# Low-rank decay input: sixteen columns taken out of the split-weight stream and multiplied in native fp32 over four column groups

## The reference, cut to what matters

```
h = modulate(rms_norm(x, norm_mix[i]), sh2, sc2)
z = h @ w_in[i]                       # 1024 x 8208 columns
ca, cb, q, k, v, r, a_lr, g_conv, g_gla = jnp.split(z, split_idx, axis=-1)
u = ca * jax.nn.sigmoid(cb)
d, conv_new = causal_depthwise_conv(u, conv_state[i], conv_w[i], conv_b[i])
log_a = jax.nn.log_sigmoid((a_lr @ w_alpha[i] + b_alpha[i]).astype(jnp.float32)) / GLA_TAU
```

## Time and profile before

| | us |
|---|---|
| median of three runs | 1552.81 |
| lowest, highest | 1550.1, 1555.76 |
| the profiled execution | 1552.72 |
| its span, first to last instruction | 1551.1 |
| PE busy in it | 1451.4 (94%) |
| DVE busy | 825.3 (53%) |
| ACT busy | 487.0 (31%) |

### The profile page before, as it was taken

How to read it: one execution, slowest core, us unless ns; L and a number is a source line. 1 busy time by engine, 2 the same in 40 slices (tenths; PEclk the granted TensorE clock), 3 DMA queues, 4 the chain that set the end, 5 groups by cost and what they waited for, 6 DMA issues and landing times. The chain is left out here.

```text
span 1551.1 us, 30240 instructions
## 1 busy us (share of the span) xinstructions
PE 1451.4 (94%) x11934; PEld 1399.7 (90%) x11934; DVE 825.3 (53%) x1381; ACT 487.0 (31%) x660; POOL 73.5 (5%) x108
## 2 busy tenths in 40 slices
PE   6999999999997998999998895899979999999996
PEld 5899999999997998998998895799979999999995
DVE  5323322332256685798795977775453343333345
ACT  5322122212235223433232233522252212222233
POOL 6100000000010000000000000000000000000000
PEclk9999999999999999999898998899989999999997
DMA  9754545454554223222323333322312322322311
GB/s 311 235 168 154 172 152 173 147 178 142 170 189 147 84 81 113 72 93 79 130 93 122 105 123 132 137 83 88 103 55 82 104 85 82 108 82 84 99 61 55
DMA packets 134277, 189.03 MB, mean 122 GB/s; under 512 B 3516, under 2 KB 114512, under 8 KB 134159
## 3 DMA queue, kind: packets, MB, share of 16 engines
q1 hardware_dynamic: 113436, 114.57, 23.3%
q0 software_dynamic: 16704, 64.75, 12.5%
q10 hardware_dynamic: 4050, 8.53, 1.5%
HBM read 174.37 MB, written 14.41 MB: 122 GB/s over the span
## 5 line engine op out<-in xcount | busy, mean ns | idle before, releaser
L1322 DVE TENSOR_TENSOR w_lo<-raw,w_hi 128x1024 fp32r<-128x1024 f32 x218 | 266.8, 1225 | 589.6 <-ACT w_hi L962 589.4
L548 PE MATMUL pu<-h_hi,w_hi 128*128 128x260 f32 x2480 | 508.1, 286 | 19.4 <-DVE w_lo L1322 10.5
L548 PE MATMUL pu<-h_hi,w_lo 128*128 128x260 f32 x2480 | 501.5, 284 | 0.0
L548 PE MATMUL pu<-h_lo,w_hi 128*128 128x260 f32 x2480 | 500.8, 284 | 0.0
L962 ACT CAST w_hi<-raw 128x1024 fp32r<-128x1024 f32 x218 | 227.9, 1046 | 682.3 <-PE pu L548 670.6
L548 PEld LDWEIGHTS pu<-h_hi,w_hi 128*128 128x128 f32 x2480 | 384.5, 190 | 27.5 <-issue 10.9
L548 PEld LDWEIGHTS pu<-h_lo,w_hi 128*128 128x128 f32 x2480 | 384.4, 190 | 0.0
L548 PEld LDWEIGHTS pu<-h_hi,w_lo 128*128 128x128 f32 x2480 | 384.3, 189 | 0.0
L1617 DVE SCALAR_TENSOR_TENSOR d<-u,cw,d 128x512 f32<-128x512 f32 x240 | 162.9, 747 | 0.0
L548 PE MATMUL pu<-f_hi,w_hi 128*128 128x260 f32 x704 | 143.0, 284 | 2.0 <-DVE f_lo L1571 2.0
L548 PE MATMUL pu<-f_hi,w_lo 128*128 128x260 f32 x704 | 141.8, 283 | 0.0
(11 more groups left out here) (260 smaller groups left out, 1242.3 us busy)
## 6 DMA issues: line engine op xcount, KB each, us to landing
raw_a<-in_w_ada POOLq DMA_DIRECT2D x32, 1024.0 KB, 7.8
raw<-in_w_in SPq DMA_DIRECT2D x30, 1024.0 KB, 5.3
raw<-in_ffn_up SPq DMA_DIRECT2D x22, 1024.0 KB, 5.3
raw<-in_ffn_gate SPq DMA_DIRECT2D x21, 1024.0 KB, 5.3
raw<-in_ffn_down SPq DMA_DIRECT2D x16, 1024.0 KB, 5.1
raw_a<-in_w_ada_final POOLq DMA_DIRECT2D x8, 1024.0 KB, 7.4
gates_d<-sg ACTq DMA_DIRECT2D x24, 260.0 KB, 2.0
raw<-in_ffn_down SPq DMA_DIRECT2D x8, 768.0 KB, 4.5
```

Of the source, the lines that this page charges most:

```text
L548: last = mm(pu[p][:, e, 0:HALF], w[p][:, k, :], m[:, k, e * HALF:(e + 1) * HALF], start=(k == 0 and j == 0), stop=(k == k_tiles - 1 and j ...
L1322: V.tensor_tensor(w_lo[p][:], raw[:, slot, :, p * P:(p + 1) * P], w_hi[p][:].bitcast(F32), ALU.subtract).then_inc(s_lo, 1)
```

## The change

`a_lr` leaves the sequence of units. Its 16 columns of `w_in` are loaded once, unsplit, into a tile `wa` of 8 k-tiles by 32 columns (16 of them zero), by one DMA that stands in SP's queue between the first feed-forward block and the conv loads. After the last conv unit PE multiplies `wa` in native fp32 (`a_rows`): k-tile k goes to column group k % 4 of the array, with the high and the low part of the activation in turn. Each group leaves its own partial sum in its own 32 PSUM partitions. ACT copies all 128 rows at once, and the logits product, whose `w_alpha` now stands four times in `walpha` with zero rows between, adds the four partial sums. POOL therefore clears `walpha` and issues four small DMAs in place of one. The four places of alr, their two weight loads, their splits on ACT and DVE and PE's wait on the last PSUM evacuation are gone.

```
-                        + [("conv", 16), ("alr", 4), ("qk", 8), ("v", 8), ("gates", 24),
+                        + [("conv", 16), ("qk", 8), ("v", 8), ("gates", 24),
...
-        walpha, alr = work[0:RANK, 0:HEADS * DK], work[0:RANK, HEADS * DK:HEADS * DK + N]
+        walpha, alr = work[:, 0:HEADS * DK], work[:, HEADS * DK:HEADS * DK + N]
+        wa = sb("wa", [P, KT, CG])
...
             ffn(1)
+            sp.wait_ge(s_wz, 1)
+            sp.dma_start(wa[:, :, 0:RANK], w_in[:, W_IN["a"]:W_IN["a"] + RANK].rearrange("(k p) n -> p k n", p=P)
+                         ).then_inc(s_wa, 16)
             with sp.Fori(0, 4) as i:
                 pair(Lin(at["conv"], 4, i), w_in, i * 256 + W_IN["cb"], (w_in, i * 256 + W_IN["ca"]))
-            pair(Lin(at["alr"]), w_in, W_IN["a"], (w_in, W_IN["a"]))
...
             pool.wait_ge(s_done, at["conv"])
-            pool.dma_start(walpha, A["w_alpha"][0]).then_inc(s_ld["wa"], 16)
+            nc.gpsimd.memset(walpha, 0.0).then_inc(s_wz, 1)
+            pool.wait_ge(s_wz, 2)
+            for g in range(4):
+                pool.dma_start(walpha[CG * g:CG * g + RANK, :], A["w_alpha"][0]).then_inc(s_ld["wa"], 16)
...
-            n = at["alr"]
-            pe.wait_ge(s_evac[1], n // 2)
-            unit(Lin(n), 0, h_hi, h_lo, done=4)
+            def a_rows():
+
+                pe.wait_ge(s_wa, 16)
+                pe.wait_ge(s_cve, KT)
+                for r in range(2):
+                    for j, m in enumerate((h_hi, h_lo)):
+                        for e in range(2):
+                            for g in range(4):
+                                last = mm(pg[CG * g:CG * (g + 1), 2 + e, 0:HALF], wa[:, 4 * r + g, :],
+                                          m[:, 4 * r + g, e * HALF:(e + 1) * HALF].bitcast(F32), start=(r == 0 and j == 0),
+                                          stop=(r == 1 and j == 1), tile_position=(0, CG * g))
+                last.then_inc(s_ao, 1)
+
+            a_rows()
...
-            n = at["alr"]
-            act.wait_ge(s_done, n + 1)
-            for e in (1, 0):
-                nc.scalar.copy(alr[:, e * HALF:(e + 1) * HALF], pu[0][0:RANK, e, 0:HALF]).then_inc(s_evac[e], 2)
-
-            for c in range(2):
-                act.wait_ge(s_raw[1], Lin(n).half().half().value(16, 16))
-                act.sem_inc(s_hi, 1)
-            for c in range(2, 4):
-                act.wait_ge(s_lo, n + c + 1)
-                step(Lin(n + c))
+            act.wait_ge(s_ao, 1)
+            nc.scalar.copy(halves(alr), pg[:, 2:4, 0:HALF]).then_inc(s_alr, 1)
...
             V.memset(c_f[:], 0.0).then_inc(s_cf, 1)
+            V.memset(wa[:], 0.0).then_inc(s_wz, 1)
...
-            n = at["alr"]
-            for c in range(2):
-                dve.wait_ge(s_raw[1], Lin(n).half().half().value(16, 16))
-                dve.wait_ge(s_hi, n + 3 + c)
-                dve.sem_inc(s_lo, 1)
-            for c in range(2, 4):
-                step(Lin(n + c))
```

More of the change, by code:

```diff
@@ L297, in decoder_step @@
         s_xsp, s_xr = sem("x_rows_spilled"), sem("x_rows_restored")
+        s_wz, s_wa = sem("w_a_cleared"), sem("w_a_loaded")
+        s_ao, s_alr = sem("a_rows_in_psum"), sem("a_rows_ready")
         s_lg, s_z, s_az = sem("logits_ready"), sem("z_ready"), sem("abs_z_ready")
@@ L746, in _ @@
                         state_transposes(4 * (c - 2))
-            n = at["alr"]
-            pe.wait_ge(s_evac[1], n // 2)
-            unit(Lin(n), 0, h_hi, h_lo, done=4)
+            def a_rows():
[10 more added lines that the diff above has]
+            a_rows()
             def u_tails():
-                pe.wait_ge(s_cve, KT)
-                pe.wait_ge(s_evac[1], at["alr"] // 2)
+                for p in range(2):
+                    pe.wait_ge(s_evac[p], at["qk"] // 2)
                 for t in range(KT):
@@ L763, in logits @@
                 if h == 0:
-                    pe.wait_ge(s_evac[0], at["alr"] // 2 + 2)
-                    pe.wait_ge(s_ld["wa"], 16)
+                    pe.wait_ge(s_alr, 1)
+                    pe.wait_ge(s_ld["wa"], 16 * 4)
                     pe.wait_ge(s_cts, 1)
@@ L1642, in _ @@
             conv.end(3)
-            n = at["alr"]
-            for c in range(2):
-                dve.wait_ge(s_raw[1], Lin(n).half().half().value(16, 16))
-                dve.wait_ge(s_hi, n + 3 + c)
-                dve.sem_inc(s_lo, 1)
-            for c in range(2, 4):
-                step(Lin(n + c))
             def sample_conv():
-                dve.wait_ge(s_evac[0], at["alr"] // 2)
-                dve.wait_ge(s_evac[1], at["alr"] // 2)
+                dve.wait_ge(s_evac[0], at["qk"] // 2)
+                dve.wait_ge(s_evac[1], at["qk"] // 2)
                 dve.wait_ge(s_cve, KT)
```

## The result

The changed kernel takes 1542.1 us (median of five runs, 1540.23 to 1545.06); the kernel before takes 1552.81 us in the same comparison (five runs, 1550.1 to 1559.12). The ratio of the two is 0.9922, with a 95% interval from 0.9899 to 0.9945: by the ratio 12 us less, and between 8.5 and 15.7; by the two medians 10.7 us less. In two later comparisons the ratio was 0.9911 (0.989 to 0.9933) and 0.9919 (0.9906 to 0.9933). The forecast was 1543.0 us.

The account below looks back on a forecast made before the run. PE, busy 94% of the span, sets the pace; the window shrinks from 19.51 us to 0.19 + 3.78 + 5.77 = 9.74, saving 9.77 from 1552.81: 1543.0 us, 8-in-10 range 1540.2 to 1546.8.

Parts of the forecast that it names:

- the window: End of last conv unit to end of first qk unit: 9.74 us in place of 19.51, saving 9.77.
- both waits: PE's idles around the alr unit, for the last PSUM evacuation (3.16 us) and first qk weights (3.25 us), both removed.
- the length of the stretch ahead: Sign: the stretch before the window (480 to 581 us) keeps its length to some tenths.
- change of form: PE switching between full-width units and `a_rows`: 0.09 us ahead and 0.10 us behind, 0.19 us added.
- the early slabs: Modulation weight slabs in the trace of before: sixteen matmuls take 1.86 us, so the 32 added ones take 3.78 us.
- the serial rival: Column groups do not overlap in `a_rows`: 15.6 us for the 32 matmuls, 1554.9 us in all; chance 0.03.
- The bound of 0.5 us for the load of `wa`: SP's queue: packets four times as dear would make the next load 1.5 us late for a cast; taken as 0.
- The 0.8 us kept for the range: POOL's `walpha` memset after the first feed-forward block: at most 0.8 us if DVE must stand still; taken as 0.
- The clock's loss in the window of before: First qk unit runs partly at 1.2 GHz, 7.25 us instead of 5.77: 1.48 us, removed by the change.
- The logits, costed at 0: Logits matmuls with 128 rows instead of 16, same 260 moving columns and matmul count: no change, 0 us.
- those that gave time back: Partly given back: lower clock level, memset and load hits in later stages cost 4.3 us, 1547.3 us; chance 0.12.
- DVE's 3.0 us of slack: DVE runs out of work 3.0 us before the first qk unit ends, so no wait returns in the v stage.

Follow-up runs that it names:

- the first repeated comparison: The changed kernel run again with no edit, beside the kernel before: 1541.83 us (six runs), ratio 0.9911 (0.989 to 0.9933).
- The second and third profile: The kernel before profiled twice more with no edit: single times 1552.38 and 1553.82 us, against 1552.81 us median of its first comparison.

## Why the prediction was right

**The path.** PE sets the pace, the window is where the change acts, and both waits go. Window 9.57 us, worked out 9.74; the same in three profiles. Of the signs, the length of the stretch ahead was claimed to some tenths. It is 0.5 us longer in the first profile of the change, and its end moves by 2.6 us over three profiles of that one program, so that sign was set too tight.

**The added matmuls.** 3.65 us with the change of form behind, worked out 3.78 + 0.10. The 1.86 us of the early slabs run to the first row of the next form, so they hold the change of form behind them; doubled, with 0.10 added, it was counted three times. The excess is 0.2 us. The 0.465 us for a group of four had it inside too; it is 0.44 with 260 columns. The 0.49 us for one logits matmul, and so the 15.6 us of the serial rival, is too large in the same way (see the logits below). Four groups overlap 3.98 times (one group against four). The Trainium skill's "TensorE: Matmul & The Clock Gate", Part 3, has 2.38 times for three groups, from which some 3.2 for four had been estimated; the measurement decides for nearly 4 in this form. The change of form itself cost 0.09 us ahead, as in the earlier trace rows. The bound of 0.5 us for the load of `wa` is not worked out: the same sentence has the load 1.5 us late. Nothing came of it.

**What was costed at 0.** The load of `wa` landed after 4.2 us, before the next weight load, and the conv loads are issued as before (453.44 us, 453.52 in the earlier trace rows). The memset on POOL lies beside DVE's residual on the path, and holds nothing up. The two timelines, POOL and DVE of the changed kernel:

```profile
471.00 0.53 POOL L498 MEMSET work<- 128x512 f32 x1 [10.79 <-PE pu L556]
```

```profile
470.97 0.49 DVE L1487 SCALAR_TENSOR_TENSOR x<-pu,mod,x 128x260 f32<-128x260 f32 x1 [0.30 <-PE pu L556]
471.38 0.47 DVE L1489 SCALAR_TENSOR_TENSOR x<-pu,mod,x 128x252 f32<-128x252 f32 x1
471.76 0.16 DVE L1491 TENSOR_TENSOR t<-pu,mod 128x8 f32<-128x8 f32 x1
```

In the kernel before, without a memset, the same three DVE operations take 0.49, 0.47 and 0.16 us. The 0.8 us kept for the range did not come. The Trainium skill's "SBUF — State Buffer", under "Who interferes with whom", has the exclusive lock for VectorE instructions in a 2-port perf mode, and says of those with two SBUF inputs that they contend with a GpSimd instruction that reads SBUF, not with one that only writes it. A memset only writes, and the trace agrees for these three operations.

**Where the size was off.** The saving was worked out as 9.77 us; the medians give 10.7 and the later ones 11.9 and 13.8 (1541.21 against 1555.04). Two terms were too small. That the forecast, 1543.0 us, still came within a microsecond of 1542.1 is in part luck: the three runs it started from have the lowest median of the kernel before, 1552.81 us, where the later comparisons have 1553.6 to 1555.0.

- The clock's loss in the window of before. I took 1.48 us, from one execution. The second and third profile have 3.1 and 4.2 us (the alr unit 7.39 and 8.49 us instead of 5.85, the qk unit 7.37 instead of 5.77). With the mean of three windows, 20.98 - 9.57 = 11.4 us. The prediction did see that one of two like waits was followed by the lower level and the other not, and drew from it only that later stages may differ, not that the window itself does.
- The logits, costed at 0. The step "a 16-row matmul takes no less than a 128-row one" is right for the matmuls and leaves out what stands round them. In the changed kernel four of them take 597.64 to 599.20:

```profile
597.40 0.40 PE L556 MATMUL pu<-h_hi,w_lo 128*128 128x260 f32 x2
597.64 1.92 PE L790 MATMUL pg<-work 128*128 128x260 f32 x8
599.20 0.59 PE L556 MATMUL pu<-h_hi,w_hi 128*128 128x260 f32 x2
599.63 0.40 PE L556 MATMUL pu<-h_lo,w_hi 128*128 128x260 f32 x2
```

From the last pair ahead to the second pair behind, that is 2.23 us, against 2.61 in the earlier trace rows (606.87 to 609.48): 0.4 us less. Narrow windows show single records. In the kernel before the second and the last of the eight are

```profile
607.52 0.38 PE L770 MATMUL pg<-work 16*128 16x260 f32 x1
608.83 0.38 PE L770 MATMUL pg<-work 16*128 16x260 f32 x1
```

and in the changed kernel the second and the sixth

```profile
597.86 0.38 PE L790 MATMUL pg<-work 128*128 128x260 f32 x1
598.74 0.38 PE L790 MATMUL pg<-work 128*128 128x260 f32 x1
```

That is 0.22 us a record in both, 1.31 over six steps and 0.88 over four: the matmuls themselves take 0.44 us each with 16 rows as with 128. The 0.4 us lies at the two ends. Before, the step to the first record is 0.32 us where a pair takes 0.24, the second record starts 0.33 us after the first, the next form 0.31 us after the last, and its first pair takes 0.34 us: 0.08 + 0.11 + 0.09 + 0.10 = 0.38. The 2.23 us now are the eight records and two steps of pairs, with nothing added. So what was saved is a change of form, from the units' 128 rows to 16 and back; with 128 rows the logits have the form of the units. I had counted such a change for `a_rows` and not the two that disappear. In the profile with one column group the logits have 32 rows, and run from 608.63 to 610.58, 1.95 us, as with 16.

The logits stand twice in the qk stage, and the second saving is partly spent in the wait of the late qk units: by the low parts of the weights, the two traces move 0.5 us further apart over the stage.

11.4 + 0.5 = 11.9 us, which is the saving of the first repeated comparison; as the three comparisons differ by 3 us, that is agreement within the noise and no more. What is left of the difference in the rest (948.6 to 950.6 us in three profiles before, 946.8 to 948.0 in three after, so 1.2 us on average beyond the logits) lies within what the same program shows; that all of it is chance is not shown.

**The rivals.** None of those that gave time back came true: behind the window PE has the same 29 waits before and after, 64.8 to 66.5 us in sum before and 65.2 to 66.8 after, and DVE's 3.0 us of slack (measured 2.9) held.

## What to carry to other kernels

A narrow product in a pipeline built for wide ones costs more in its places in the pipeline than in its matmuls: here 6.4 us of waits and 1.5 to 4.2 us of clock, beside 5.85 us of matmuls. Taken out of the sequence it needs no buffers of the pipeline, and can stand wherever PE is idle; put into such an idle, it cost 3.4 us less than at its old place, 2.2 of them on PE's path. A burst of another form also costs something at its two ends (0.3 to 0.4 us here), which a row read from its start to the next form's start already contains. And a term that comes from the granted clock of one profile is a sample: take its range from several stretches or executions before adding it up.

## What the runs showed of the hardware

- Four native fp32 matmuls with 32 stationary columns each, issued in turn to four column groups, take 0.44 us together, as long as one alone (14.15 us for 32 in one group, 3.65 in four), although each has its own weights and the activation changes every time.
- Native fp32 matmuls of 260 columns take 0.44 us each, with 16 rows as with 128. A burst of them between fp32r units costs 0.38 us more with 16 rows than with the units' own 128 rows (2.61 us against 2.23 for four), and the starts of the single records put it at the ends of the burst; with 32 stationary columns the two ends cost about 0.3 us (4.32 us from the last pair ahead, 581.19, to the second pair behind, 585.51; the matmuls and two steps of pairs make 4.0).
- Two waits of 3.16 and 3.25 us round one unit were followed by the lower clock level after one of the two in one execution and after both in two others, with the same program and the same length of the waits to 0.1 us.
